# The up-projection's units 62 to 121: high and low tokens in one product of 448 columns, the halves added by a DMA of GpSimd

## The reference

```
sc = einsum('bshpd,phnd->bshpn', q, keys)          # two sets of 128 scores for each of 8 heads
v1, i1 = top_k(sc[..., 0, :], 16);  v2, i2 = top_k(sc[..., 1, :], 16)
best, pos = top_k(v1[:, None] + v2, 16)            # 16 of 256 pairs
idx = i1 * 128 + i2 of those;  gates = softmax(best)
act = gelu(einsum('tkd,td->tk', u[idx], h), approximate=False)
out = einsum('tk,tkd->td', gates * act, v[idx])
```

## Time and profile before

| | |
|---|---|
| median of 3 runs | 1386.96 us (1385.44 to 1388.8) |
| profiled execution, its own time | 1385.96 us |
| its span in the trace | 1383.9 us |
| what lies around the span | 2.06 us |
| units 62 to 121 | from about 431 to 606.5 us of the span |

### The profile page before, as it was taken

One profiled execution on the slowest core, in us unless ns is written; L12 is line 12 of the kernel. 1 busy time (PEld: TensorE's weight loads), 2 busy tenths in 40 slices (PEclk: granted clock), 3 DMA queues, 4 the chain that ended last, 5 costly groups with the idle time before them and its releaser, 6 DMA issues.

```text
span 1383.9 us, 26738 instructions
## 1 busy us (share of the span) xinstructions
PE 1360.1 (98%) x10953; PEld 1290.8 (93%) x10953; DVE 1035.8 (75%) x1844; ACT 737.7 (53%) x1077; POOL 293.5 (21%) x176
## 2 busy tenths in 40 slices
PE   9999999999999999999999999999999999999997
PEld 7989989999999999999999999999898798899985
DVE  5556575593987899989999878987677664777744
ACT  5674645545464444444444556555677554655533
POOL 6000000288873222220000033220232000100000
PEclk9999999999999999999999999999999999999999
DMA  7434366456569777775555689986343543555552
GB/s 246 145 130 129 119 195 212 139 199 198 195 225 329 281 238 253 250 248 184 183 190 185 203 323 347 347 298 233 128 147 107 183 151 115 177 184 186 188 189 91
DMA packets 76585, 279.26 MB, mean 202 GB/s; under 512 B 8496, under 2 KB 8752, under 8 KB 76208
## 3 DMA queue, kind: packets, MB, share of 16 engines
q1 hardware_dynamic: 67104, 243.73, 52.6%
q0 software_dynamic: 9216, 33.56, 6.5%
q10 hardware_dynamic: 144, 0.26, 0.1%
HBM read 276.47 MB, written 1.05 MB: 201 GB/s over the span
## 4 chain that ended last, share of the span: by engine, by line
PE 75%; issue 15%; ACT 5%; DVE 4%; POOL 1%; DMA 0%; POOLq 0%; SPq 0%; DVEq 0%; ACTq 0%
PE bank L476 74%; ACT A L1227 2%; ACT whi L1227 2%; DVE wlo L1805 2%; PE bank L485 1%; POOL wlo L2713 1%; ACT L1227 1%; DVE A L1805 1%; DVE A L1801 0%; DMA xres<-in_x 0%; DVE xres L1805 0%; ACT hT L1227 0%; DVE small L2514 0%; DVE small L1805 0%; POOL small L2719 0%
## 5 line engine op out<-in xcount | busy, mean ns | idle before, releaser
L476 PE MATMUL bank<-hT,whi 128*128 128x224 f32 (+2 forms) x5148 | 1008.9, 294 | 2.7 <-DVE wlo L1805 1.7
L476 PEld LDWEIGHTS bank<-hT,whi 128*128 128x128 f32 x5148 | 811.7, 190 | 19.1 <-DVE wlo L1805 2.5
L476 PE MATMUL bank<-hT,wlo 128*128 128x224 f32 (+1 forms) x2952 | 810.5, 275 | 0.0
L1227 ACT ACTIVATE whi<-raw 128x1024 fp32r<-128x1024 f32 (+1 forms) x450 | 473.1, 1053 | 353.4 <-PE bank L476 346.1
L1805 DVE TENSOR_TENSOR wlo<-raw,whi 128x1024 fp32r<-128x1024 f32 (+1 forms) x385 | 471.8, 1227 | 225.2 <-ACT whi L1227 224.9
L476 PEld LDWEIGHTS bank<-hT,wlo 128*128 128x128 f32 x2952 | 562.7, 191 | 0.0
L1227 ACT ACTIVATE A<-bank 128x512 f32<-128x512 f32 (+4 forms) x170 | 90.2, 537 | 218.9 <-PE bank L476 209.2
L2713 POOL TENSOR_TENSOR wlo<-raw,whi 128x1024 fp32r<-128x1024 f32 x63 | 150.9, 2413 | 150.9 <-ACT whi L1227 148.3
L2719 POOL TENSOR_TENSOR small<-small 128x1 f32<-128x1 f32 x16 | 9.8, 614 | 491.1 <-DVE small L1802 487.3
L2729 POOL DMA_INDIRECT A<-in_v,small x32 | 51.2, 1599 | 287.8 <-DVE A L1801 174.1
L2729 POOL DMA_INDIRECT A<-in_utab,small x32 | 53.6, 1675 | 133.4 <-DVE A L1808 131.9
(11 more groups left out here) (181 smaller groups left out, 1292.3 us busy)
## 6 DMA issues: line engine op xcount, KB each, us to landing
raw<-in_u SPq DMA_DIRECT2D x128, 512.0 KB, 3.4
raw<-in_v SPq DMA_DIRECT2D x128, 512.0 KB, 3.9
raw<-in_w_up SPq DMA_DIRECT2D x44, 512.0 KB, 3.2
raw<-in_w_down SPq DMA_DIRECT2D x22, 512.0 KB, 3.3
raw<-in_w_in_t SPq DMA_DIRECT2D x17, 512.0 KB, 3.5
raw<-in_w_in_g SPq DMA_DIRECT2D x16, 512.0 KB, 3.3
raw<-in_w_out SPq DMA_DIRECT2D x16, 512.0 KB, 3.7
raw<-in_w_pq SPq DMA_DIRECT2D x16, 512.0 KB, 4.2
```

Of the source, the lines that this page charges most:

```text
L476: return e.matmul(o, l, r, start=st, stop=sp_, skip_group_check=True)
L1227: return e.activation(o, i, func, **kw)
```

## The change

PE (`wide`): units 62 to 121 take one product of 448 columns (high weights by high and low tokens) and one of 224 (low weights by high tokens) for each k. The 448 columns fill a bank for one unit: the first 224 hold two of the three sums, the others the third. So a bank now serves one unit instead of two, by `4 + u % 3`, and is free when ACT has copied it out (`u_ev`).

ACT: `take_wide(n)` copies the 448 columns of unit n in two halves, to slots n and n + 4 of `acts` (`B_AHEAD`), without GELU. `gelu_wide(n)` takes the GELU of slots n and n + 1 in place, in iteration n + 5, once the halves have been added.

POOL (`add_halves`): at each even unit u it waits for the copies of units u - 2 and u - 1 and issues one DMA that adds slots n + 4, n + 5 onto n, n + 1 (n = u - 2), 128 rows of 1792 bytes (224 KB), SBUF to SBUF. There are 30 of them, and three semaphores in turn.

Units 122 to 127 are as before, but their GELU (`gelu_pair`) comes up to two iterations later.

```diff
+WIDE = (62, 122)
+B_AHEAD = 4
...
+        def halves_added(n):
+            k = (n - WIDE[0]) // 2
+            return s[f"u_add{k % 3}"], 16 * (k // 3 + 1)
...
+            def wide(u0, u1):
+                both = t4(hT[:, :], 2, KD)
+                for u in range(u0, u1):
+                    wv = two(unit(BASE["u"] + u), KD)
+                    bk = banks[4 + u % 3]
+                    use(4 + u % 3)
+                    for k in range(KD):
+                        mm(bk[:, 0:2 * TD], wv[0][:, k, :], both[:, :, k, NG:T], k == 0, False)
+                        ins = mm(bk[:, 0:TD], wv[1][:, k, :], both[:, 0, k, NG:T], False, k == KD - 1)
+                    ins.then_inc(s["w"], 1)
+                    free[4 + u % 3] = (s["u_ev"], u - WIDE[0] + 1)
+                    pair[0] += u % 2
+                    side.step()
...
-            lin_T(BASE["u"] + 62, G_DENSE - 62, hTv, KD, c0=NG)
+            wide(WIDE[0], G_DENSE)
             side.lists[0] += [gates(0), gates(1)]
-            lin_T(BASE["u"] + G_DENSE, P - G_DENSE, hTv, KD, c0=NG)
+            wide(G_DENSE, WIDE[1])
+            lin_T(BASE["u"] + WIDE[1], P - WIDE[1], hTv, KD, c0=NG)
...
-            def first_cuts(u):
-                if u == 64:
+            def take_wide(n):
+                if n == WIDE[0]:
+                    e.wait_ge(s["rt_dve"], 8)
+                if TD * (n + B_AHEAD + 1) > 16896:
+                    e.wait_ge(s["pk_used"], EARLY)
+                e.wait_ge(s["w"], BASE["u"] + n + 1)
+                act(acts[:, n:n + B_AHEAD + 1:B_AHEAD, :], t3(banks[4 + n % 3][:, 0:2 * TD], 2), ACT.Copy
+                    ).then_inc(s["u_ev"], 1)
+
+            def gelu_wide(n):
+                e.wait_ge(*halves_added(n))
+                z = acts[:, n:n + 2, :]
+                act(z, z, ACT.Gelu).then_inc(s["ev_act"], 1)
+                pair[0] += 1
+
+            def gelu_pair(n):
+                e.wait_ge(s["w"], BASE["u"] + n + 2)
+                gelu(n)(0, t3(banks[4 + pair[0] % 3][:, :], 2))
+                pair[0] += 1
+
+            for u in range(WIDE[0], P):
+                hi(BASE["u"] + u + 2)
+                if u % 2 and WIDE[0] <= u - 5 < WIDE[1]:
+                    gelu_wide(u - 5)
+                if u <= WIDE[1] and u > WIDE[0]:
+                    take_wide(u - 1)
+                if u % 2 and u - 3 >= WIDE[1]:
+                    gelu_pair(u - 3)
+                if u == 126:
                     cut_acts(0)
                     cut_acts(1)
-
-            lin_T(BASE["u"] + 62, 66, gelu(62), first_cuts)
+                side.step()
+            gelu_pair(126)
...
+            def add_halves(n):
+                e.wait_ge(s["u_ev"], n - WIDE[0] + 2)
+                sem, count = halves_added(n)
+                e.dma_start(acts[:, n:n + 2, :], acts[:, n + B_AHEAD:n + B_AHEAD + 2, :], accum_op=ALU.add
+                            ).then_inc(sem, 16)
+
...
                     for g in GATHERS.get(u, ()):
                         gather(g)
+                    if WIDE[0] < u <= WIDE[1] and u % 2 == 0:
+                        add_halves(u - 2)
```

More of the change, by code:

```diff
@@ L172 @@
 own_act own_dve own_pool zeros x_sq hi_half lo_half lo_first f_xg f_xd f_act hd_mask
-pk_idx pk_rep pk_used pk_act v_tile v_b v_sum v_tr
+pk_idx pk_rep pk_used pk_act v_tile v_b v_sum v_tr u_ev u_add0 u_add1 u_add2
 """.split()
```

## The result

The changed kernel takes 1389.32 us (median of 11 runs, 1387.19 to 1392.45), the kernel before 1385.67 us in the same comparison (11 runs, 1385.44 to 1388.8). The ratio is 1.0021 with a 95% interval of 1.0013 to 1.0030. So it is slower, by 0.2%, where 1379.8 us was forecast; 1390.0 was the upper end of the range.

What follows compares the result with a forecast made beforehand. PE was taken to bound this stretch. Shorter steps -9.6, stall at unit 122 +1.4 and first adds +1.0 gave -7.2 us, from 1386.96 to 1379.8; own range 1376 to 1383, widened to 1375.5 to 1390.

Steps and rivals of the forecast that it cites:

- stall at unit 122: PE at unit 122 waits for ACT's copy of unit 121 out of bank 5: +1.4 us, once.
- the first adds: First add on POOL stands behind gather 9: ACT 3.4 us late, PE 0.4; with the next ones +1.0 us (0 to 3).
- four later places: Where gathers stand right before an add on POOL, 1.93 us at most; ACT's slack takes it, no cost.
- L: Time from ACT's copy of a pair's second unit to the sum's landing, POOL's queue included; taken as 6 us.
- late adds as a rival: Rival: L over 8.6 us in most pairs, adds delaying ACT and PE; with L = 10, 1401 us; chance 0.20.
- bounds worked out for L: ACT waits for an add only from L of 7.9 us, PE is held up for good only from 8.6.
- The gain: PE, units 62 to 121: 480 products fewer, steps of 0.315 for 0.335 us: 9.6 us (8.6 to 10.6).
- rival that the wide product gives nothing: Rival: PE's step stays 0.335 us and only the stalls are left, +2.4 us, 1389.4; chance 0.05.
- The DMA's price: Adding DMA of 224 KB, nearest to a gather, lands in 6 us; a plain copy in 3 to 4.
- ACT at no cost of its own: ACT's two more copies make 3.75 us of a 5.61 us pair: no cost.
- DVE not the bound: DVE falls behind 0.6 us at most against 0.84 of slack: no cost; rival that it binds, 1383 us, chance 0.14.
- bandwidth: DMA traffic of 313 to 354 GB/s in the changed units is covered, if thinly.

Runs made afterwards that it cites:

- kernel without adds: Changed kernel with the adding DMAs and every wait for them left out: median 1380.70 us, ratio 0.9954 against the kernel before; stretch 184.02 us.
- adds first: Changed kernel with POOL's adds ahead of the gathers and gathers 9 to 31 one unit later: median 1382.65 us, ratio 0.9972 against before.
- copies without the sum: Changed kernel with the 30 DMAs copying in place of adding, same places and waits: median 1385.30 us, ratio 0.9989 against before.
- mended version with the same order: Changed kernel with adds ahead of gathers, four slots ahead, new form only up to unit 119: median 1382.33 us, ratio 0.9969 against before.
- same traffic without waits: Changed kernel with 30 same-size accumulating DMAs from an idle tile into free slots, no GELU waiting: median 1381.58 us, ratio 0.9964 against before.

## Why the prediction was wrong

In the profiled executions, each term beside its forecast:

| term | forecast, us | measured, us | from |
|---|---|---|---|
| shorter steps | -9.6 | -7.7 | 190.33 - 184.02 = 6.31, and 1.40 of stall |
| stall at unit 122 | +1.4 | +1.4 | 1.89 - 0.49 |
| late adds | +1.0 | +6.8 | 190.82 - 184.02 |
| tail | none | +2.1 | 6.8 - 4.7 |
| rest of the run | none | +0.8 | 0.46 ahead, 0.37 behind |
| sum | -7.2 | +3.4 | span 1387.3 - 1383.9 |

The 0.8 has no cause in the change that a run showed; starts of the stretch differ by up to 2.1 us between kernels that are alike up to there (431.5 to 433.6), and the time from its end to the last output by 3.2 us (756.9 to 760.2).

**The step that failed** is "the first adds", with its last sentence on the four later places, "L is then 8 to 9 for one pair, which ACT's slack takes". The mechanism was in it: an add behind a gather that waits for a dot, issued 5.9 us into unit 64, and so it was (442.74; unit 64 began at about 436.7). The sizes were not. The add's data landed 7.9 us after its issue where I had reckoned with about 6, so the GELU started 13.9 us into unit 64 and not 12. The next add, behind the next gather, took 9.8. PE so waited 2.06 us for the bank of unit 66, where 0.4 was forecast. And I priced this one wait alone. Behind a late GELU ACT's `whi` is late, then DVE's `wlo`, and DVE, whose slack I had put at 0.84 us for another purpose, then hands over `og` late: five more waits of PE. "ACT's slack" was not the nearest; DVE's was. Against the kernel without adds, the GELU of units 72 and 73 was 3.9 us behind (476.53 against 472.67), that of units 120 and 121 7.1 (618.03 against 610.91), of both of which 0.32 is the later start of the stretch: 3.5 of the 6.80 us came with the first adds, that of 464.35 among them, which is one of the four later places, and 1.5, 1.1 and 0.6 at the three others. That order decides, **adds first** shows (184.02); that the length of an accumulating DMA decides with it, **copies without the sum** shows (184.23). Each alone takes the loss away.

**The late adds as a rival** (0.20) had the right cause and the right sign, but not the form: L was not over 8.6 in most pairs, as it wanted; a GELU waited for its add 8 times in 30, behind gathers and in the wake of the first of them. In **adds first** the first GELU starts 7.3 us after its add's issue (438.69 to 446.00), GELUs wait by up to 0.9 us, and none of them holds PE; in the mended version with the same order the landings are 4.8 / 6.9 / 8.0 us (least, median, most). The bounds worked out for L (ACT waits from 7.9, PE from 8.6) agree with that.

**The gain** was mis-sized by 1.9 us, because the model form stands in a stage whose operand has another start. Had the columns of the tokens started at a multiple of 256, 190.33 - 181.88 + 1.40 = 9.85 us would have come, where 9.6 was forecast. In the Trainium skill (TensorE: Matmul & The Clock Gate, Back-to-back issue gap) the price of the removed product would be 2.5 ns, 1.2 us in all; the trace differs, with 7.7 us. The same section calls that formula the gap of an isolated product, without a budget for the weight load, and a weight load went with each of these products; for the start column it has no term. The rival that the wide product gives nothing is out.

**The DMA's price** was taken between rows that were no adds: 6 us, with 7.2 as measured. The Trainium skill (Collectives: The Full Stack, "Why ReduceScatter is half of AllGather") has two source reads for an add and so half the rate; here 7.2 stands against 4.5 for a copy, a factor of 1.6 in time, so the direction agrees and the size doesn't quite.

**Right** were the stall at unit 122 (1.40, as forecast), ACT at no cost of its own, DVE not the bound (no `og` wait without adds), and bandwidth: 313 GB/s was reckoned with, 354 with the second reads; 310 moved in the same traffic without waits, at a share of 0.99, and PE waited for nothing but the copy at unit 122. (The profile counts an add's bytes once: 279.26 MB before, 286.09 with 30 adds of 224 KB, so 310 stands beside 313.) **Missing** was the tail: no term of the sum asked what a DMA of GpSimd costs outside the place where it is issued.

**Three figures** of the prediction don't follow from its own terms, and none of them moves the forecast. The lower end of the forecast's own range is 1386.96 - 10.6 + 1.4 = 1377.8, not 1376. With L = 10 the time is 1386.96 + 13.4 + 1.4 = 1401.8, not 1401. And at L = 9.1 the same line gives 1388.3; 1390 stands for an L near 9.2.

## What to carry to other kernels

Before a transfer is put into an in-order queue, look at what stands ahead of it there and what that waits for: an instruction with a deadline goes ahead of those that wait for buffers. When a wait is predicted, follow it to every engine behind it and compare with the smallest slack on the way, not with the first. When one trace holds a form to be copied, compare also the start columns of its operands.

## What the runs showed that I had not expected

- An accumulating DMA of 224 KB from SBUF to SBUF lands in 7.2 us (median) where a plain one lands in 4.5, and POOL spends 0.90 us on issuing it in place of 0.55.
- Each direct DMA that GpSimd issued here lengthened the end of the program by about 0.07 us, long after it had landed: 4.7 us with none, 5.9 with 15, 6.8 with 30. Why is open.
- With token columns that start 32 behind a multiple of 256, a step of two products (448 and 224 columns) took about 4.5 ns more than with columns that start at the multiple; where the result starts in the bank (0 or 32) made no difference.
- DMA engines busy for 0.99 of 169 us held up PE nowhere.
- GpSimd's add of 128x448 nearly doubled a dot product of DVE beside it, 1.22 to 2.18 us. The Trainium skill (GPSIMD Engine Reference, Specifications) has the SBUF interfaces shared with VectorE where its instruction has two SBUF inputs, and the dot product has two; the trace agrees.
